# Rotating the projected keys and queries: partners copied by ScalarE out of PSUM, the first angle table ahead of the modulation sums, the index scores one unit earlier

## What is computed

```python
ang = positions[..., None] * freqs                  # theta 10000
cos, sin = jnp.cos(ang), jnp.sin(ang)
x1, x2 = x[..., :half], x[..., half:]
return concatenate([x1 * cos - x2 * sin, x2 * cos + x1 * sin])
```

## Time and profile before

| | us |
|---|---|
| median of 3 runs | 700.03 (698.43 to 700.11) |
| the profiled execution, its own time | 697.74 |
| span of that execution, first to last instruction | 695.9 |
| PE busy in the span | 629.8 |
| DVE busy | 370.4 |
| ACT busy | 167.3 |
| POOL busy | 71.9 |
| mean granted TensorE clock, share of full | 0.972 |

### The profile page before, as it was taken

The page is one execution under the profiler, slowest core; times in us unless marked ns, Lnnn a source line. Parts: engine busy times, 40 slices in busy tenths (PEclk is TensorE's granted clock), DMA queues, the critical chain, the costliest instruction groups (busy, mean ns, idle before and its releaser), DMA issues.

```text
span 695.9 us, 7082 instructions
## 1 busy us (share of the span) xinstructions
PE 629.8 (91%) x2400; PEld 295.4 (42%) x2400; DVE 370.4 (53%) x742; ACT 167.3 (24%) x342; POOL 71.9 (10%) x75
## 2 busy tenths in 40 slices
PE   0598999959999999999989999989999999988983
PEld 0374444424444444446554456433434453433331
DVE  4777254987888675325984335872332333232055
ACT  1340000122423333441012223111212222221022
POOL 1001021110011111000000000112111111110101
PEclk9999999979999999999999999999999999998997
DMA  9993948080341819053089317899999999999996
GB/s 313 394 317 96 316 118 271 23 265 0 107 151 36 267 32 310 9 192 89 1 333 379 133 60 307 299 395 408 419 421 419 419 419 420 420 418 413 408 406 139
DMA packets 56532, 179.94 MB, mean 259 GB/s; under 512 B 10800, under 2 KB 11312, under 8 KB 45616
## 3 DMA queue, kind: packets, MB, share of 16 engines
q1 hardware_dynamic: 45136, 160.26, 60.4%
q0 software_dynamic: 6160, 12.10, 5.4%
q10 hardware_dynamic: 5200, 7.12, 3.8%
HBM read 168.43 MB, written 15.21 MB: 264 GB/s over the span
## 4 chain that ended last, share of the span: by engine, by line
PE 72%; DMA 10%; DVE 8%; issue 4%; SPq 3%; ACT 2%; ACTq 1%; POOL 0%; POOLq 0%; DVEq 0%
PE psum L1052 14%; PE psum L772 14%; PE psum L775 11%; PE psum L1113 8%; PE psum L920 7%; DMA both_bufs<-pair_rows 3%; DMA ring<-in_w_ada 2%; PE psum L1025 2%; SPq L647 2%; PE psum L877 2%; DMA both_bufs<-both_bufs 2%; PE psum L897 2%; PE psum L885 1%; PE psum L851 1%; PE psum L905 1%
## 5 line engine op out<-in xcount | busy, mean ns | idle before, releaser
L772 PE MATMUL psum<-hT,ring 128*128 128x512 f32 (+1 forms) x320 | 136.6, 581 | 2.3 <-DVE both_bufs L1517 2.3
L1052 PE MATMUL psum<-ring,hT 128*64 128x512 f32 (+2 forms) x320 | 92.2, 594 | 1.9 <-DMA ring<-in_w_up_exp 1.6
L772 PEld LDWEIGHTS psum<-hT,ring 128*128 128x128 f32 x320 | 60.4, 193 | 71.9 <-issue 60.7
L775 PE MATMUL psum<-ring,hT 128*128 128x512 f32 x192 | 87.1, 607 | 0.0
L1874 DVE TENSOR_SCALAR work<-work 128x256 f32<-128x256 f32 x16 | 4.6, 290 | 101.8 <-PE psum L1062 76.0
L775 PEld LDWEIGHTS psum<-ring,hT 128*128 128x128 f32 x192 | 36.4, 194 | 45.8 <-issue 45.6
L1454 DVE SCALAR_TENSOR_TENSOR rows<-ring,sm,rows 128x512 f32<-128x512 f32 x64 | 49.1, 767 | 8.7 <-DMA rows<-in_b_ada 7.1
L1052 PEld LDWEIGHTS psum<-ring,hT 128*64 128x64 f32 (+2 forms) x320 | 31.7, 142 | 49.0 <-issue 46.3
L1342 ACT ACTIVATE work<-psum 128x256 f32<-128x256 f32 x17 | 6.5, 384 | 146.6 <-PE psum L1052 146.6
L1113 PE MATMUL psum<-ring,work 128*64 128x512 f32 (+1 forms) x160 | 40.1, 598 | 0.7 <-ACT work L1348 0.7
L1052 PE MATMUL psum<-both_bufs,hT 128*64 128x512 f32 x64 | 31.1, 643 | 3.5 <-issue 3.5
(11 more groups left out here) (309 smaller groups left out, 867.0 us busy)
## 6 DMA issues: line engine op xcount, KB each, us to landing
ring<-in_w_down_exp SPq DMA_DIRECT2D x20, 1024.0 KB, 18.6
ring<-in_w_in SPq DMA_DIRECT2D x8, 2048.0 KB, 10.6
ring<-in_w_ada SPq DMA_DIRECT2D x8, 2048.0 KB, 15.6
ring<-in_w_gate_exp SPq DMA_DIRECT2D x14, 1024.0 KB, 21.7
ring<-in_w_up_exp SPq DMA_DIRECT2D x14, 1024.0 KB, 24.4
ring<-in_w_ada SPq DMA_DIRECT2D x7, 1024.0 KB, 14.2
ring<-in_w_gate_exp SPq DMA_DIRECT2D x12, 512.0 KB, 14.9
ring<-in_w_up_exp SPq DMA_DIRECT2D x12, 512.0 KB, 15.1
```

What stands on the lines that cost most here:

```text
L772: mm = pe.matmul(o[:, at], w[:, k, b * P:(b + 1) * P], hT3[:, k, at], start=(k == 0), stop=(k == KD - 1))
L775: mm = pe.matmul(o[:, :], hT3[:, k, b * P:(b + 1) * P], w[:, k, :], start=(k == 0), stop=(k == KD - 1))
L1052: mm = pe.matmul(o[rows, :], XT[u % 2][:, k, rows], both(GU_SLOT[place])[:, k, :, :], start=(k == 0), stop=(k == KD - 1))
```

## The change

- The partner half is no longer made by DVE's sine product and DMAs. ACT copies it straight out of the PSUM bank (`swap`: four copies of 32 partitions for a unit, two of 64 for qr and kr) and counts `swapped`. POOL multiplies it by the sine table (whose sign is now that of the receiving half) and then adds it to the destination. DVE keeps the cosine product, which waits for ACT's copies, so that `rope_ab` still says that the bank has been read.
- ACT's copies stand at the unit's own step, ahead of the index scores of that step, where the DMA issues stood at `sums`.
- The first table is made ahead of all sums: DVE computes its angles before the first chunk, ACT takes its sines before the first square root. The second table: DVE in the step `sums` of kw, ACT in the step `sums` of ka 0.
- The index scores begin behind ka 0, one unit earlier, and end behind va 3 and no longer behind qr 0.
- The load of the decay rows on SP's queue waits for `roped` of kr 3, where it waited for `rope_ab`.

```diff
-        c[:, C_TRIG + 2 * n + 1] = np.where(i // half % 2 == 0, 1.0, -1.0)
+        c[:, C_TRIG + 2 * n + 1] = np.where(i // half % 2 == 0, -1.0, 1.0)
...
-        idx_from, att_from, ret_from = units.index(("ka", 1)), units.index(("va", 0)), units.index(("gr", 0))
+        idx_from, att_from, ret_from = units.index(("ka", 0)), units.index(("va", 0)), units.index(("gr", 0))
...
-                    sp.wait_ge(rope_ab, len(plan.rope))
+                    sp.wait_ge(roped, len(plan.rope))
...
+            def sines(n):
+                act.wait_ge(ang_ready, n + 1)
+                a.activation(trig[n][:, 1, :], trig[n][:, 1, :], ACT.Sin, bias=zero,
+                             scale=cst[:, C_TRIG + 2 * n + 1:C_TRIG + 2 * n + 2]).then_inc(trig_ready, 1)
+                a.activation(trig[n][:, 0, :], trig[n][:, 0, :], ACT.Sin).then_inc(trig_ready, 1)
+
             act.wait_ge(cst_in, 16)
+            sines(0)
...
-                act.wait_ge(rope_ab, r + 1)
+                act.wait_ge(unit_done, plan.unit[s] + 1)
+                if kind == "kw":
+                    a.activation(head_wts, bank(s)[DH:KW, :], ACT.Copy).then_inc(kw_out, 1)
                 if r >= 2:
                     act.wait_ge(roped, r - 1)
                 rows = pieces(kind)
                 for n, here in enumerate(rows):
                     there = rows[(n ^ 1) % 2] if kind == "kw" else rows[n ^ 1]
-                    act.dma_start(SWAPPED[r % 2][here, at], CROSS[r % 2][there, at]).then_inc(swapped[r % 2], 16)
+                    ins = a.activation(SWAPPED[r % 2][here, at], bank(s)[there, at], ACT.Copy)
+                ins.then_inc(swapped, 1)
...
-                elif s[0] == "sums" and s[1] in TURNED:
-                    swap(("unit",) + s[1:])
+                elif s == ("sums", "ka", 0):
+                    sines(1)
...
+            dve.wait_ge(pos_in, 16)
+            link(v.tensor_copy(posf, posi))
+            angles(0)
...
-                dve.wait_ge(unit_done, plan.unit[s] + 1)
+                dve.wait_ge(swapped, r + 1)
                 dve.wait_ge(trig_ready, 2 * table + 2)
-                if r >= 2:
-                    dve.wait_ge(roped, r - 1)
...
-                v.tensor_tensor(CROSS[r % 2][rows, at], o, trig[rows, table, 1, at], ALU.mult).then_inc(rope_ab, 1)
+                ins.then_inc(rope_ab, 1)
...
                     kind, b = s[1:]
-                    if kind != "kw" and b < NB - 1:
+                    if kind == "kw":
+                        dve.wait_ge(x_n, NB)
+                        angles(1)
+                    elif b < NB - 1:
...
+                pool.wait_ge(trig_ready, 2 * table + 2)
+                pool.wait_ge(swapped, r + 1)
+                g.tensor_tensor(other, other, trig[table][:, 1, at], ALU.mult).then_inc(crossed, 1)
+                pool.wait_ge(crossed, r + 1)
                 pool.wait_ge(rope_ab, r + 1)
-                pool.wait_ge(swapped[r % 2], swaps_to(r))
-                g.tensor_tensor(dst, dst, SWAPPED[r % 2][:, at], ALU.add).then_inc(roped, 1)
+                g.tensor_tensor(dst, dst, other, ALU.add).then_inc(roped, 1)
```

More of the change, by code:

```diff
@@ L306, in build @@
         into = {"qi": qiT, "ka": kaT, "qa": qaT}
[L307 to L310, removed]
+        trig = [home.rearrange("p (f t) -> p f t", f=2) for home in (ropebuf[:, 0:2 * S], xs[:, 2048:2048 + 2 * S])]
         SWAPPED = [ropebuf[:, (2 + i) * S:(3 + i) * S] for i in range(2)]
+        posi = SWAPPED[0].bitcast(I32)
+        posf, turns = T2[:, 0:S], T2[:, S:2 * S]
         decay = xs[:, 2048:4096].rearrange("p (h t) -> p h t", h=RHEADS)
@@ L1222, in _ @@
                              scale=gs1[:, k:k + 1]).then_inc(x_evA, 1)
[L1223 to L1227, removed]
             act.dma_start(G1, prow(t["g_post_mix"], D)).then_inc(post_in, 16)
@@ L1249, in _ @@
                     a.activation((vr if name == "vr" else va)[:, b, :], bank(s)[:, :], ACT.Copy).then_inc(v_ready, 1)
-                elif s == ("unit", "kw", 0):
-                    act.wait_ge(unit_done, plan.unit[s] + 1)
-                    a.activation(head_wts, bank(s)[DH:KW, :], ACT.Copy).then_inc(kw_out, 1)
+                elif s in plan.rope:
+                    swap(s)
                 elif s[0] == "unit" and s[1] == "gr":
@@ L1459, in ada, with angles @@
                     ins.then_inc(ada_done, 1)
[L1461 to L1474, removed]
+            def angles(n):
+                cos, sin = trig[n][:, 0, :], trig[n][:, 1, :]
+                link(v.tensor_scalar(sin, posf, cst[:, C_TRIG + 2 * n:C_TRIG + 2 * n + 1], None, ALU.mult))
+                link(v.tensor_scalar(turns, sin, 1.0 / (2 * math.pi), MAGIC, ALU.mult, ALU.add))
+                link(v.tensor_scalar(turns, turns, MAGIC, None, ALU.subtract))
+                for part in TWO_PI:
+                    link(v.scalar_tensor_tensor(out=sin, in0=turns, scalar=-part, in1=sin, op0=ALU.mult, op1=ALU.add))
+                link(v.tensor_scalar(sin, sin, 3.1415925, -3.1415925, ALU.min, ALU.max))
+                link(v.scalar_tensor_tensor(out=cos, in0=sin, scalar=-1.0, in1=sin, op0=ALU.mult, op1=ALU.min))
+                v.tensor_scalar(cos, cos, math.pi / 2, None, ALU.add).then_inc(ang_ready, 1)
+            dve.wait_ge(pos_in, 16)
+            link(v.tensor_copy(posf, posi))
+            angles(0)
             for i in range(RING):
@@ L1493, in _ @@
                                 ALU.add).then_inc(x_evV, 1)
-            angles()
             def rotate(s):
@@ L1513, in rotate @@
                 o = bank(s)[rows, at]
[L1514 removed]
+                ins = v.tensor_tensor(dst[rows, at], o, trig[table][rows, 0, at], ALU.mult)
                 if kind == "kw":
[L1516 to L1517 removed]
+                    ins = v.tensor_tensor(dst[DH:2 * DH, :], o, trig[table][rows, 0, :], ALU.mult)
+                ins.then_inc(rope_ab, 1)
             def mask_of(b):
@@ L1996, in rotate @@
                 dst = (kiT if kind == "kw" else into[kind][:, b, :])[:, at]
+                other = SWAPPED[r % 2][:, at]
+                table = 1 if kind in ("qr", "kr") else 0
+                pool.wait_ge(trig_ready, 2 * table + 2)
+                pool.wait_ge(swapped, r + 1)
+                g.tensor_tensor(other, other, trig[table][:, 1, at], ALU.mult).then_inc(crossed, 1)
+                pool.wait_ge(crossed, r + 1)
                 pool.wait_ge(rope_ab, r + 1)
-                pool.wait_ge(swapped[r % 2], swaps_to(r))
-                g.tensor_tensor(dst, dst, SWAPPED[r % 2][:, at], ALU.add).then_inc(roped, 1)
+                g.tensor_tensor(dst, dst, other, ALU.add).then_inc(roped, 1)
             def bias(m):
```

8 lines of the change are left out of this document (2 added, 6 removed).

## The result

The changed kernel's median is 695.05 us (20 runs, 690.71 to 701.99), that of the kernel before, run beside it, 699.88 us (20 runs). The ratio is 0.9939, with an interval of 0.9913 to 0.9965: 0.6% faster, 4.3 us by the ratio and 4.8 by the medians. The sign and the range (688.0 to 696.5) held. The size did not: -9.1 us were forecast, and about half came.

The account below looks back on a forecast made before the run. PE was taken as the bound, 72% of the span. +1.0 - 2.27 - 1.75 + 1.3 - 7.61 - 1.88 + 0.3 = -10.9 us; with a 1.8 us clock charge -9.1, so 690.9 us from 700.03, range 688.0 to 696.5.

Parts of the forecast that it names:

- The three removals: PE's 2.27 us idle ahead of qi 2, 1.75 of slow matmuls behind; 7.61 ahead of attention scores, 1.88 behind: all go.
- The wait of 7.61: PE's idle ahead of the first attention scores, for qa 3's rotation: gone whole, -7.61 us, and 1.88 of slow unit behind.
- The meeting of POOL and DVE: In each qa unit, POOL's addition beside DVE's two-operand sums costs DVE 0.9 us.
- the cycle of a qa unit: DVE's time on a qa unit, 8.68 us before: 8.98 each for qa 1 and qa 2.
- the port costs DVE the whole addition: Rival, qa units: DVE loses 1.27 us a meeting, clock falls at MOD 2 and MOD 3, 694.2 us; chance 0.17.
- both of POOL's passes hold it: Rival: POOL's two passes hold DVE wherever they fall, so the kernel is slower, 703.4 us at 4.0 a meeting; chance 0.04.
- the expert stream sets the end: Rival, expert stage from 418 us: the order of weight loads is the bound, gain lost in waits, 700 us; chance 0.06.
- I charge one fall, 1.8 as in rows 2, for the two together: PE's idle stretches at MOD 2 (1.9 us) and MOD 3 (1.35 or more) together cost one clock fall, 1.8 us.
- MOD 2: PE's wait ahead of MOD 2: ACT copies for 2.04 us first, so it starts 1.3 us later, bounds 0 and 3.3.
- MOD 3: PE's wait ahead of MOD 3: DVE arrives 64.45 us after qa 0's end, idle 1.35 instead of 1.10, +0.3 us.
- Start: First unit, behind the sums: making the first angle table ahead of them delays it, +1.0 us, bounds 0.7 and 1.7.

Follow-up runs that it names:

- experiment 4: Changed kernel with POOL's addition of the turned half left out, so the rotation is incomplete: 694.84 us, one run.
- Experiment 1: Changed kernel with two steps of filler matmuls each ahead of MOD 2 and MOD 3: 690.52 us, ratio 0.9898.
- 11: Changed kernel with ka 3's partner copies behind the relus, one selection round moved behind kr, filler matmuls ahead of MOD 3 and of the attention-output turns: 689.28 us.
- experiment 5: Changed kernel with the partner copies of unit ka 3 moved behind the relus on ScalarE: 694.37 us, ratio 0.9924.
- Experiment 7: Changed kernel with one warm-up step instead of three ahead of the first turns: 698.17 us, ratio 0.9973.
- experiment 10: Changed kernel with filler matmuls ahead of MOD 2, MOD 3 and the turns of the attention's output: 690.98 us, ratio 0.9871.

## Why the prediction was right or wrong

**Right: what goes.** The three removals came as worked out. From the first unit to kw's start the changed kernel is 2.70 + 1.57 = 4.27 us shorter (forecast 2.27 + 1.75 = 4.02). The wait of 7.61 and the slow unit behind it are gone whole; 0.68 us for a relu stand there instead. The meeting of POOL and DVE costs 0.89 (forecast 0.9), the cycle of a qa unit in the changed kernel is 9.09 and 8.96 (8.98). The rivals in which the port costs DVE the whole addition, or both of POOL's passes hold it, fall with experiment 4's comparison, though the first of them charged both falls and its 694.2 lies closest to the measured median: right number, wrong mechanism; the one in which the expert stream sets the end falls with experiments 1 and 11, whose leads reach the end of the kernel.

**Wrong: "I charge one fall, 1.8 as in rows 2, for the two together".** This is the step that failed. Two stretches, two falls: 1.74 + 2.98 = 4.7 us in the profiled run, 2.9 more than charged. Experiment 1 takes the idle from TensorE without shortening a wait and gets the clock back in both places. Over all profiles of kernels with these two waits, an idle stretch of 2.34 or 2.35 us at MOD 2 lost the clock six times in six, 2.3 to 2.4 us at MOD 3 four times in five, 1.42 us at MOD 3 three times in three; 0.4 to 1.1 us at these two places never did. I had set the falls against each other as if they were one event because rows 4 had a stretch with no fall. That was one draw, and its length was misread: the window 363 to 367 cuts it to 1.7 us, but the row has 2.31, longer than the 2.27 that took the clock.

```profile
364.63 2.58 PE L868 MATMUL psum<-cst,work 128*128 128x128 f32 x16 [2.31 <-DVE work L1824]
```

The same 2.31 us stands there in ten profiles without filler, before's included, and the clock fell behind it in six of them, for 0.9 to 2.9 us. So length does not decide it, and what does no run shows. How many falls the median run of the changed kernel has is not known either: eleven of its 20 runs have a mean clock of 0.981 to 0.985 and take 690.7 to 695.6 us, the profiled one has 0.970.

**Sizes that were off.**
- MOD 2: idle +1.78 instead of +1.3. Four 32-partition copies from PSUM take 2.38 us, 0.595 apart, where 2.04 were taken from the 0.48 behind a first relu. The bounds held it (0 for copies that cost a quarter, 3.3 for double ones), and experiment 5 shows that the whole of it was avoidable.

```profile
102.81 2.38 ACT L1243 ACTIVATE both_bufs<-psum 32x512 f32<-32x512 f32 x4 [4.63 <-PE psum L768]
105.22 0.66 ACT L1264 ACTIVATE both_bufs<-psum 128x256 f32<-128x256 f32 x2
```

- MOD 3: idle 2.32 instead of 1.35, since DVE came 66.0 us behind qa 0's end, not 64.45. Of these 1.56 us, 0.31 are its later start on qa 0 (it waits for the copies, 2.46 behind the unit), 0.49 qa 0 itself, 0.09 the next two, and 0.66 lie behind the start on qa 3, in it and the va units. TensorE came later too (63.7 against 63.1), so the idle grew by only 1.0. With the fall, this is the costliest term: forecast +0.3 and half a fall, measured +1.2 and 2.98.
- Start: +1.57 instead of +1.0. DVE's first sum came at 13.24 (forecast 13.65) and its last ended at 37.02, as before; the loss is not in the sums. Before idled 2.21, 0.46 and 0.48 us between them, and all of it was there to take up the later start; now DVE works without a gap from 13.24 to 37.02. The late sums push six warm-up matmuls, 5.25 us, to 33.11, between the column sums and the turns. In the kernel before they filled a gap, since the turns behind them still waited for ScalarE (timeline of PE before); now they stand in the way. Experiment 7 shows 1.1 us of it. And 1.57 is a lucky figure: in before's profile the last twenty turns ran into a fall (3.99 us from the first of them to the first unit, granted clock 0.50 from 40 to 42), in the changed kernel's they did not (2.96).

```profile
29.71 4.40 PE L803 MATMUL psum<-cst 128*128 128x512 f32 x6
34.71 0.94 PE L815 MATMUL psum<-cst,work 128*128 128x128 f32 x6 [0.61 <-ACT work L1206]
...
39.04 4.20 PE L815 MATMUL psum<-cst,work 128*128 128x128 f32 x20
```

The change also put the landing of the positions on the path. Over the twelve profiles with the table ahead DVE begins it at 7.09 to 8.97 us, and from some 7.6 us on, where its gaps are used up, the end of the sums moves with it one for one (37.02 for 7.63, 37.93 for 8.53, 38.36 for 8.97). With the falls over the turns the first unit starts anywhere from 43.85 to 47.20 us in the ten of them with three warm-up steps.

Terms against terms at 195 us, in the profiled runs: -9.1 + 2.9 (falls) + 0.6 (start) + 0.5 (MOD 2) + 1.0 and 0.6 (MOD 3, VectorE and TensorE) = -3.5, measured -4.1; the rest, 0.6, is spread over small steps and not assigned.

**Left open.** Why the runs of one kernel spread by 4 to 11 us. The time goes with the granted clock (in the repeat of the changed kernel, 0.980 to 0.982 in three of its five fastest runs, 0.967 to 0.971 in the six slowest), and the places where it fell differ from profile to profile: the last turns ahead of the first unit, MOD 2, MOD 3, near 360, and near 425 us, where MOD's product takes 2.9 to 3.8 us in all thirteen. From the 160-column product behind it (434.74 in after) to the end it is 261.7 to 264.5 us in all of them, so the expert stage is not where they mainly part. Taking away the fall near 360 (experiment 10) did not narrow the spread. The turns at the start and the place near 425 were not filled.

## What to carry to other kernels

When a change removes a large wait, list every idle stretch of TensorE that it leaves or makes, with its length, and charge each a clock fall of its own (0.9 to 3.1 us here), weighted by how often it came in the profiles of such a stretch: above 1.4 us in 19 of 24, 1.1 us and less at MOD 2 and MOD 3 in none. Take the length from the instruction's row, since a window can cut it. Then remove the stretch by order, or fill it with matmuls on a bank that is free anyway. Work put on an engine with slack still has a place in its queue: look for what stands directly behind it on that engine and who waits for that, here two relus of 0.66 us that four copies pushed out by 1.8. Where runs fall in two groups, compare profiles stage by stage, look whether a place of unchanged code lost the clock in one of the two, and check one stage's effect in a second profile of the same kernel before giving it a cause.

## What was not expected of the hardware

Copies of 32 partitions from a PSUM bank cost as much as of 128: four of 512 columns take 2.38 us, 0.595 each, where one of 128 partitions takes 0.60, so four quarter copies cost four whole ones. Over all 68 copies on ScalarE, 16 of them of 384 columns and 16 of 64 partitions, the median is 0.587 us (0.479 to 0.597). The clock fell behind only 1.42 us of idle in three profiles of three, and did not fall behind 2.34 us in one, in the same kernel in which it had. And behind stretches of the same 2.32 us at MOD 3 a fall cost 1.4 us in experiment 5 and 3.1 in experiment 7 (3.75 and 8.29 us for the two blocks).
